# The last block's sums joined in PSUM instead of added in DRAM, and the last blocks moved out of the loop

## The reference, cut to what matters

```python
def moe(x, router_w, router_bias, w_gate, w_up, w_down):
    x2 = x.reshape(-1, D_MODEL)                      # 1088 x 1024
    gates = route(x2, router_w, router_bias)         # 2 of 16 experts per token
    out = jnp.zeros(x2.shape, jnp.float32)
    for e in range(N_EXPERTS):
        h = jax.nn.silu(x2 @ w_gate[e]) * (x2 @ w_up[e])      # 512 columns
        out = out + gates[:, e:e + 1] * (h @ w_down[e])
    return out
...
x = layer_norm(DN_ALPHA * x + moe(x, ...), ln2_g, ln2_b)
```

## Time and profile before

| | |
|---|---|
| median of 3 runs | 1126.72 us (1123.49 to 1126.98) |
| the profiled execution's own time | 1126.72 us |
| its span, first to last instruction | 1125.0 us |
| PE busy | 1034.6 us (92%) |
| DVE busy | 682.2 us (61%) |
| ACT busy | 527.7 us (47%) |
| mean granted TensorE clock | 0.961 |

### The profile page before, as it was taken

The page is one execution under the profiler, slowest core; times in us unless marked ns, Lnnn a source line. Parts: engine busy times, 40 slices in busy tenths (PEclk is TensorE's granted clock), DMA queues, the critical chain, the costliest instruction groups (busy, mean ns, idle before and its releaser), DMA issues. The chain is left out here.

```text
span 1125.0 us, 18261 instructions
## 1 busy us (share of the span) xinstructions
PE 1034.6 (92%) x5572; PEld 846.3 (75%) x5573; DVE 682.2 (61%) x1345; ACT 527.7 (47%) x902; POOL 245.2 (22%) x586
## 2 busy tenths in 40 slices
PE   7999999999899999999987999999999999999820
PEld 5877879789576765788866788888888888888710
DVE  4548467341699726476547646654576789686437
ACT  4233333432588747322212335644475678565324
POOL 0623655900200100000000113322232322224100
PEclk9999999999799999999998999999999999999965
DMA  7230241203760064733322778667878899997355
GB/s 242 64 102 29 72 124 44 70 24 102 241 208 2 9 204 132 287 117 125 126 75 75 266 262 269 222 196 227 284 251 309 279 356 389 341 344 237 107 163 192
DMA packets 53555, 201.66 MB, mean 179 GB/s; under 512 B 11410, under 2 KB 17426, under 8 KB 47346
## 3 DMA queue, kind: packets, MB, share of 16 engines
q1 hardware_dynamic: 42978, 138.50, 34.8%
q0 software_dynamic: 7488, 27.49, 10.3%
q10 hardware_dynamic: 3024, 34.87, 7.9%
HBM read 164.02 MB, written 36.81 MB: 179 GB/s over the span
## 5 line engine op out<-in xcount | busy, mean ns | idle before, releaser
L2150 DVE TENSOR_TENSOR wlo<-raw,whi 128x1024 fp32r<-128x1024 f32 x192 | 221.8, 1219 | 37.9 <-ACT whi L2047 33.2
L2047 ACT ACTIVATE whi<-raw 128x1024 fp32r<-128x1024 f32 x184 | 179.3, 1049 | 31.0 <-PE psG L1989 13.5
L1987 PE MATMUL psY<-whi,ehs 128*128 128x512 f32 x200 | 81.0, 405 | 4.1 <-DVE wlo L2150 4.1
L1987 PE MATMUL psG<-whi,exs 128*128 128x512 f32 x200 | 80.5, 402 | 2.1 <-DVE exs L2155 2.1
L1948 POOL DMA_INDIRECT acc<-eyb,idxs x25 | 41.3, 1653 | 181.0 <-ACT eyb L2065 181.0
L1989 PE MATMUL psY<-whi,ehs 128*128 128x512 f32 x200 | 78.9, 395 | 0.0
L1988 PE MATMUL psY<-wlo,ehs 128*128 128x512 f32 x200 | 78.6, 393 | 0.0
L1989 PE MATMUL psG<-whi,exs 128*128 128x512 f32 x200 | 78.2, 391 | 0.0
L1989 PE MATMUL psU<-whi,exs 128*128 128x512 f32 x200 | 78.0, 390 | 0.0
L1988 PE MATMUL psG<-wlo,exs 128*128 128x512 f32 x200 | 77.9, 390 | 0.0
L1987 PE MATMUL psU<-whi,exs 128*128 128x512 f32 x200 | 77.8, 389 | 0.0
(11 more groups left out here) (396 smaller groups left out, 2335.2 us busy)
## 6 DMA issues: line engine op xcount, KB each, us to landing
raw<-in_moe_w_gate SPq DMA_DIRECT2D x16, 2048.0 KB, 9.7
raw<-in_moe_w_up SPq DMA_DIRECT2D x16, 2048.0 KB, 11.1
raw<-in_moe_w_down ACTq DMA_DIRECT2D x16, 2048.0 KB, 9.9
early<-in_w_in SPq DMA_DIRECT2D x27, 256.0 KB, 3.5
stg<-in_x_prompt SPq DMA_DIRECT2D x8, 512.0 KB, 4.5
kc<-in_cache_k SPq DMA_DIRECT2D x16, 256.0 KB, 3.1
vc<-in_cache_v SPq DMA_DIRECT2D x16, 256.0 KB, 3.0
mr<-in_w_out SPq DMA_DIRECT2D x8, 512.0 KB, 3.3
```

The costliest lines, as they stand in the source:

```text
L1987: pe.matmul(out, hi, w_hi, start=(k == 0), stop=False)
L2047: nc.scalar.activation(whi[:, at], s.raw[:, at], ACT.Copy).then_inc(hi_made[i], 1)
L2150: nc.vector.tensor_tensor(wlo[:, at], s.raw[:, at], whi[:, at].bitcast(F32), ALU.subtract) \
```

## The change

Four things are changed, all at the end.

First, `over_blocks` runs the loop for one pair less, and the last two blocks in straight code behind it: block 23 as before and block 24 by a function `last` of each engine. There PE's order is gate of 24, down of 23, up of 24, turning of h, down of 24; x is not turned for a block 25.

Second, the last block's rows are not added in DRAM. SP loads acc when the add of block 23 has landed. ACT and DVE scale and split psY into a high part yh and a low part yl. DVE makes a 0/1 matrix `whose` from the slots' token numbers: its column n of block b is 1 where a slot is token n of that block. For each token block, PE puts the loaded rows into PSUM by a product with the identity (`carry`, plain float32, 512 columns twice) and adds the last block's rows by `whose` times yh and yl (`join`, four products of 512 columns).

Third, the sums lie in three PSUM tiles in turn (psX, psGU, psY), and the statistics and the first normalising pass read them there. `carry(b)` waits until the first pass of block b-3 has been made.

Fourth, psG and psU are halves of one tile psGU, and ACT's scratch for the sums is yb[0] instead of yb[1].

```diff
+        psGU = c.enter_context(nc.psum_tensor("psGU", [P, 2 * FE], F32))
+        psG, psU = psGU[:, 0:FE], psGU[:, FE:2 * FE]
...
+        yh, yl = xs[1]
+        whose = wlo[:, 0:NBLK * P]
...
+        whole = [psX[:, :], psGU[:, :], psY[:, :]]
+        joined = [[whole[b % 3][:, h * 512:(h + 1) * 512] for h in range(2)] for b in range(NBLK)]
+        def over_blocks(eng, block, last):
...
-                with eng.If(bb <= more):
+                with eng.If(bb < more):
                     pair(bb)
+            block(2 * more + 1, 1, more + 2)
+            last(2 * more + 2)
             return more
...
+                for i in range(2):
+                    sp.wait_ge(lo_made[i], 4 * top + 4)
                 sp.wait_ge(all_added, 1)
+                sp.wait_ge(added, 32 * more + 32)
                 for b in range(NBLK):
+                    if b == QB:
+                        sp.wait_ge(lo_made[2], 4 * top + 4)
+                        sp.wait_ge(loads_in, 1)
                     r = rows(b)
                     sp.dma_start(z[b][0:r, :], s.acc[b * P:b * P + r, :]).then_inc(z_in[b], 16)
...
-                more = over_blocks(pe, block_)
-                down(2 * more + 2, 0)
+                def last(b):
+                    done = 4 * entry(pe, 1, b, 1, E) + 1
+                    pe.wait_ge(x_split, b + 1)
+                    pe.wait_ge(act_done, b)
+                    product(psG[:, :], xs[0], KD, lambda k: GATE_AT + k * FE,
+                            lambda c: pe.wait_ge(lo_made[0], done + c)).then_inc(g_made, 1)
+                    down(b - 1, 1)
+                    product(psU[:, :], xs[0], KD, lambda k: UP_AT + k * FE,
+                            lambda c: pe.wait_ge(lo_made[1], done + c)).then_inc(gu_made, 1)
+                    turn_h(b, 0)
+                    down(b, 0)
+
+                over_blocks(pe, block_, last)
+
+                def carry(b):
+                    pe.wait_ge(z_in[b], 16)
+                    if b >= 3:
+                        pe.wait_ge(weighted, b - 2)
+                    for h in range(2):
+                        pe.matmul(joined[b][h], s.ident[0:rows(b), :], z[b][0:rows(b), h * 512:(h + 1) * 512],
+                                  start=True, stop=False)
+
+                def join(b):
+                    for h in range(2):
+                        at = slice(h * 512, (h + 1) * 512)
+                        pe.matmul(joined[b][h], whose[:, b * P:(b + 1) * P], yh[:, at], start=False, stop=False)
+                        last = pe.matmul(joined[b][h], whose[:, b * P:(b + 1) * P], yl[:, at], start=False, stop=True)
+                    last.then_inc(z_made, 1)
+
+                carry(0)
+                carry(1)
+                pe.wait_ge(y_split, 1)
+                for b in range(NBLK):
+                    join(b)
+                    if b + 2 < NBLK:
+                        carry(b + 2)
...
+                    keep_y(b - 1, 1)
+                    keep_h(b, 0)
+                    with act.If(entry(act, 2, b, 0, 1) > 0):
+                        high(b, 2, (y_made, b))
+
+                more = over_blocks(act, block_, last)
+                act.wait_ge(y_made, 2 * more + 3)
+                act.wait_ge(slots_kept, 4 * more + 6)
+                nc.scalar.activation(yh[:, :], psY[:, :], ACT.Copy, scale=gcol[:, 0:1]).then_inc(y_high, 1)
...
-                    act.wait_ge(z_in[b], 16)
+                    act.wait_ge(z_made, b + 1)
...
+                ch(nc.vector.tensor_copy(slot_of[:, :], idxs[:, :]))
+                ch(nc.vector.tensor_scalar(slots_at[:, :], s.count[:, 0:NBLK], -float(P), slot_of[:, 0:1], ALU.mult, ALU.add))
+                ch(nc.vector.tensor_tensor(whose.rearrange("p (b n) -> p b n", b=NBLK), mid(s.count[:, :], NBLK),
+                                           wide(slots_at[:, :], P), ALU.is_equal))
+                dve.wait_ge(y_high, 1)
+                nc.vector.scalar_tensor_tensor(yl[:, :], psY[:, :], gcol[:, 0:1], yh[:, :].bitcast(F32),
+                                               ALU.mult, ALU.subtract).then_inc(y_split, 1)
...
+                    dve.wait_ge(z_made, b + 1)
+                    nc.vector.scalar_tensor_tensor(zb, whole[b % 3][0:r, :], mean[0:r, b:b + 1], s.lg2[0:r, :], ALU.subtract, ALU.mult)                         .then_inc(weighted, 1)
```

More of the change, by code:

```diff
@@ L1847, in experts @@
         gate_kept, gate_next = sem("ex_gate_kept"), sem("ex_gate_next")
-        psG = c.enter_context(nc.psum_tensor("psG", [P, FE], F32))
-        psU = c.enter_context(nc.psum_tensor("psU", [P, FE], F32))
+        psGU = c.enter_context(nc.psum_tensor("psGU", [P, 2 * FE], F32))
+        psG, psU = psGU[:, 0:FE], psGU[:, FE:2 * FE]
         psY = c.enter_context(nc.psum_tensor("psY", [P, D], F32))
         psX = s.psX
+        yh, yl = xs[1]
+        whose = wlo[:, 0:NBLK * P]
+        slot_of, slots_at = sb("slot_of", [P, 1]), sb("slots_at", [P, NBLK])
         psH = c.enter_context(nc.psum_tensor("psH", [P, FE], F32))
@@ L1869, in experts @@
         z_in = [sem(f"co_z{b}") for b in range(NBLK)]
-        def over_blocks(eng, block):
+        y_high, y_split, z_made = sem("co_y_high"), sem("co_y_split"), sem("co_z_made")
+        whole = [psX[:, :], psGU[:, :], psY[:, :]]
+        joined = [[whole[b % 3][:, h * 512:(h + 1) * 512] for h in range(2)] for b in range(NBLK)]
+        def over_blocks(eng, block, last):
             more = eng.value_load(s.more_pairs[0:1, 0:1], min_val=USED_PAIRS - 1, max_val=NSB // 2 - 3)
@@ L1911, in _ @@
                     sp.wait_ge(w_in[i], 16 * E)
-                sp.wait_ge(loads_in, 1)
+                top = entry(sp, 1, NSB, 1, E)
+                more = sp.value_load(s.more_pairs[0:1, 0:1], min_val=USED_PAIRS - 1, max_val=NSB // 2 - 3)
+                for i in range(2):
+                    sp.wait_ge(lo_made[i], 4 * top + 4)
                 sp.wait_ge(all_added, 1)
+                sp.wait_ge(added, 32 * more + 32)
                 for b in range(NBLK):
+                    if b == QB:
+                        sp.wait_ge(lo_made[2], 4 * top + 4)
+                        sp.wait_ge(loads_in, 1)
                     r = rows(b)
@@ L1935, in gather, with slots @@
                         .then_inc(gathered[j], 16)
-                def add_rows(b, j):
+                def slots(b):
                     if from_block(b, 1):
@@ L1944, in add_rows @@
                     pool.wait_ge(slots_kept, 2 * b + 2)
+                def add_rows(b, j):
+                    slots(b)
                     pool.wait_ge(y_kept, b + 1)
@@ L1961, in block_ @@
                         add_rows(b - 1, 1 - j)
[L1963 to L1966, removed]
+                def last(b):
+                    r = entry(pool, 1, b, 1, E)
+                    e = pool.value_load(s.order[0:1, bass.ds(r - 1, 1)], min_val=0, max_val=E - 1)
+                    pool.wait_ge(x_turned, b + 1)
+                    nc.gpsimd.tensor_copy(s.slot_gate[:, bass.ds(b, 1)], xg[0][:, bass.ds(D + e, 1)]).then_inc(gate_kept, 1)
+                    pool.wait_ge(gate_kept, b + 1)
+                    pool.sem_inc(gate_next, 1)
+                    add_rows(b - 1, 1)
+                    slots(b)
+                more = over_blocks(pool, block_, last)
+                pool.sem_inc(all_added, 1)
+                pool.wait_ge(gathered[0], 16 * more + 32)
                 pool.wait_ge(gathered[1], 16 * more + 32)
-                pool.sem_inc(all_added, 1)
             @block.tensor
@@ L2111, in block_, with last @@
                         high(0, 2)
-                more = over_blocks(act, block_)
-                keep_y(2 * more + 2, 0)
+                def last(b):
+                    act.wait_ge(g_made, b + 1)
+                    act.wait_ge(act_done, b - 1)
+                    nc.scalar.activation(th[0][:, :], psG[:, :], ACT.Tanh, scale=0.5).then_inc(tanhed, 1)
+                    with act.If(entry(act, 3, b - 1, 0, 1) > 0):
+                        r, count = entry(act, 0, b - 1, 1, E - 1), entry(act, 1, b - 1, 1, E)
+                        act.wait_ge(lo_made[2], 4 * count + 4)
+                        load_down(r)
+                    keep_y(b - 1, 1)
[6 more added lines that the diff above has]
+                nc.scalar.activation(yh[:, :], psY[:, :], ACT.Copy, scale=gcol[:, 0:1]).then_inc(y_high, 1)
                 loads = entry(act, 0, NSB, 1, E)
@@ L2121, in act_stats @@
                 def act_stats(b):
-                    act.wait_ge(z_in[b], 16)
-                    junk = yb[1][:, :]
+                    act.wait_ge(z_made, b + 1)
+                    junk = yb[0][:, :]
                     n = ACT_STATS.index(b) + 1
@@ L2127, in act_stats @@
                         act.wait_ge(act_var, n - 1)
-                    nc.scalar.activation(junk, z[b][:, :], ACT.Copy, scale=-1.0 / (32 * D), accum_out=part[:, b:b + 1]) \
+                    tile = whole[b % 3]
```

(24 more changed lines are left out.)

7 lines of the change are left out of this document (3 added, 4 removed).

## The result

The changed kernel takes 1139.86 us (1138.12 to 1141.77) against 1126.85 beside it: a ratio of 1.0125, 95% interval 1.0104 to 1.0146. The forecast was 1132.0, its range 1127 to 1137.5. The direction was right; the loss, 13.0 us, is more than twice the forecast's.

What follows compares the result with a forecast made beforehand. PE was taken to bound the kernel up to the last product, then a relay, then DVE from its first statistics. Terms +1.2 − 8.9 + 0.2 + 12.9 = +5.4 on 1126.72 gave 1132.1, stated as 1132.0; range 1127 to 1137.5.

Steps and rivals of the forecast that it cites:

- the price of the identity product: PE's tail products putting loaded rows into PSUM: 0.45 us per 128x512 product, 0.90 per block at full clock.
- the identity product is dearer: Rival on PE's tail: 0.91 us per 128x512 identity product instead of 0.45, sum about 1139; chance 0.03.
- C: Part from DVE's first statistics to the end of its last pass: forecast +13.1 us.
- A and B: Parts from block 1's tanh to ACT's last-product copy, and from there to first statistics: forecast +1.2 and −8.9 us.
- The bare turns and the order: Ahead of the last product: unused loop turns leave PE bare, +1.5 us; new gate, down, up order, −0.3.
- From the product to the statistics: Between last product and DVE's first statistics: 3.7 us instead of 12.6, so −8.9.
- The hand-over of PSUM: Normalising chain: DVE waits for sums ahead of blocks 2, 4 and 6; 8.2 us extra at full clock.
- The clock: PE behind the last product: both clock levels in each burst, 12.9 us as the middle of 8.2 and 17.6.
- If the last product also ran at full clock … 1124: Side case of the clock rival: last product takes 5.56 us instead of 7.4, giving 1124.
- half clock to the end: Rival: PE's tail at half clock, 17.6 us, and turns bare, 3.65; 1139; chance 0.09, including more turns bare.
- the clock holds: Rival: PE stays at 1.00 behind the last product, 8.2 instead of 12.9 us, 1127.4; chance 0.20.
- DVE is fed after all: Rival on the normalising chain: PE or ACT faster out of PSUM than any row, 1120 to 1123; chance 0.06.

Runs made afterwards that it cites:

- the clock held: Changed kernel with 7, 9 and 9 spare identity products in PE's waits ahead of the identity products of blocks 3, 5 and 7: 1131.84 us, ratio 1.0044.
- the order alone: Kernel before with only the new order and the loop left one pair earlier, the add in DRAM kept: 1127.8 us, ratio 1.0003.
- half the identity product: Changed kernel with the identity product made for the first 512 columns only: 1131.93 us, ratio to before 1.004.
- each join at once: Changed kernel with blocks 0 and 1 joined first, then each block's 0/1 products right behind its own identity product: 1124.2 us, ratio 0.9991.
- the fourth tile: Kernel with each block's 0/1 products right behind its identity product, plus a fourth PSUM tile for the sums: 1117.8 us, ratio 0.992.
- double identity products: Changed kernel with each identity product issued twice, the second over the first: 1152.87 us, ratio 1.0239.
- after: Profiled execution of the changed kernel, set against the kernel before: 1139.86 us measured for that kernel, ratio 1.0125.
- the changed kernel again: Changed kernel as it is, measured a second time against the kernel before: 1137.23 us, ratio 1.0122.
- holding the clock there: Fourth-tile kernel with 8 spare identity products ahead of the last product: 1118.72 us with the new order, 1117.51 us with before's loop.

## Why the prediction was wrong, point by point

**The failed step is the price of the identity product**, "so I take 0.45", and the 0.90 per block that follows from it. Rows 5 show 11 records 0.224 apart, and I took a record for a product. It is half of one: 0.45 us for 256 columns, 0.86 for 512, 1.72 for a block. The trace of before could have told. The row of rows 5 was read in a window that began inside a burst; the whole burst, which line 1692 issues as `keep_busy(pe, s, 10)`, ten products, shows as

```profile
592.10 6.38 PE L1622 MATMUL spare<-identz 128*128 128x256 f32 x20 [1.37 <-PEq L1278]
```

The rival "the identity product is dearer" named the price and 1139, and got 0.03; its mechanism was what happened. Its argument against was the same misread row. That its time fits so well is in part luck: by its own terms C would be +20.0 (8.4, three times 0.9, and 8.9 for the clock as the middle of both levels), 2.2 more than measured, and A and B together are 2.0 longer than forecast. By the rows now a plain f32 product of 512 columns costs 0.86 us against 0.227 for each of the split products. The Trainium skill (FP8 and Floating Point Precision, TensorE Precision Notes) says that true FP32 takes four passes; the traces come near that, with 3.8 times the split product's time.

What the size did, in C: 8.4 us is the forecast at full clock. With the clock held C is +12.1, so the dearer product costs 3.7 there (0.82 in each of three groups, 0.6 ahead of block 1's statistics, which wait 0.84 where 0.2 was forecast; 0.6 is not assigned). The half clock adds 5.7, where I had 4.7: it doubles a dearer product, but mostly the first one after each wait, and not half of all work behind the waits. 8.4 + 3.7 + 5.7 = 17.8.

**The bare turns and the order** were right: +1.53 and −0.36 where +1.5 and −0.3 were forecast, A +1.2 in the order alone and +1.3 to +1.4 in the kernels with half the identity product, each join at once and the fourth tile. Both executions of the changed kernel, though, have +2.5 and +2.7, that with spare products in the waits +2.8 and that with double identity products +1.8, with psG of block 23 at the same distance. The start of the last product runs at half clock for longer there: 0.50 over 4.1 us in after (1072.3 to 1076.4) and over 6.1 us in the changed kernel again and with spare products in the waits, against 0.54 over 3.7 us with the fourth tile. In after, 0.5 us more lies ahead of block 24's gate product, where PE waits for DVE's split of x. Why either happens in some executions and not in others stays open; the forecast had no term for it.

**From the product to the statistics**: −8.1 instead of −8.9. The identity products of blocks 0 and 1, four of 512 columns, take 3.44 us and end at 1083.60, 0.8 after DVE's low part; at 0.45 each they were to be hidden beside ACT and DVE. With half of them B is 0.47 shorter.

**The hand-over of PSUM** was right as a mechanism: three idle stretches of DVE, at the places named, ended by ACT's sums or the 0/1 products. The experiments show what of it was avoidable: 12.9 us by PE's order, with the clock that this kept, and 5.6 more by a fourth tile.

**The clock**: both levels in each burst, as forecast. "If the last product also ran at full clock … 1124" was wrong: holding the clock there gains 0.2 to 0.7, since DVE's splits feed that product piece by piece.

**The other rivals**: "half clock to the end" gives about the measured time for the wrong reason (the clock is 1.00 in a good part of each burst); "the clock holds" is true only of the kernels with spare products in the waits or with each join at once, and "DVE is fed after all" only of those with the fourth tile.

## What to carry to other kernels

Before you price an instruction by a row, hold the row's count against the number that the code issues, over a whole burst and not a window that begins inside it: two records per product halved the price of the term that decided. Where tiles are handed back and forth, write down what the engine does between "tile free" and "sums ready"; one product of another block there cost 12.9 us over three groups, of which 5.7 is the clock that went with the longer waits. Compare parts of an execution from a row that the change doesn't touch, not spans.

## What the hardware showed that I had not expected

- A plain f32 product of 128x512 with the identity as weights leaves two records and takes 0.86 us at full clock; a split product of the same size leaves one and takes 0.227.
- The clock after PE's waits in the tail: 1.00 after waits of 1.43 to 1.93 us (each block joined at once), 0.50 to 0.57 after those of 3.30 to 4.57 us (after). It need not be low at once: with half of the identity product, after the same wait of 3.30 us, it was 0.95 for 1.1 us and then 0.50 for 1.7.
- A half-speed PE need not cost anything: the last product took 7.4 us from its start to ACT's copy at mixed clock (fourth tile) and 7.2 at full clock, with DVE as its feed.
- The two executions of the changed kernel are 2.8 us apart at the tanh of block 1, past the middle of the span, and all thirteen are 5.8 apart, though the change leaves the code up to there as it was. The distance from there to psG of block 23 repeats to 0.2 us in all with the new order (383.22 to 383.38) and to 0.3 in those with before's loop (381.73 to 382.07).
